# A hybrid decoder layer on one core: a narrow group norm, early small loads, and the sample's third score part moved forward

## The reference

```
sp = einsum('bqhcd,bkhcd->bhcqk', q, k_past) * ATT_SCALE      # sample: 1024 past keys out of pages
sn = einsum('bqhcd,bkhcd->bhcqk', q, k) * ATT_SCALE           # and 4 new ones
p = softmax(concatenate([sp, sn], axis=-1), axis=-1)
wgt = p[:, :, 0] - lam * p[:, :, 1]                           # differential attention, prompt and sample alike
o = einsum('bhqk,bkhd->bqhd', wgt, v)
o_att = rmsnorm(o, g_subln) * (1.0 - lam_init)
...
mean = mean(y, axis=-1)                                       # y: (tokens, 8 heads, 64) of the RWKV group
var = mean(square(y - mean), axis=-1)
y = ((y - mean) * rsqrt(var + GN_EPS)).reshape(b, t, D_RWKV)
y = y * ln_x_w + ln_x_b
y = (y + bonus) * g
mix = concatenate([o_att, y], axis=-1) @ w_o
```

## Time and profile before

| | us |
|---|---|
| runs | 2062.02, 2064.7, 2070.59 |
| median | 2064.7 |
| the profiled execution's own time | 2063.8 |
| its span, first to last instruction | 2062.0 |
| TensorE busy in the span | 1852.0 |
| VectorE busy | 1078.5 |
| ScalarE busy | 810.7 |
| GpSimd busy | 292.7 |

### The profile page before, as it was taken

The page is one execution under the profiler, slowest core; times in us unless marked ns, Lnnn a source line. Parts: engine busy times, 40 slices in busy tenths (PEclk is TensorE's granted clock), DMA queues, the critical chain, the costliest instruction groups (busy, mean ns, idle before and its releaser), DMA issues.

```text
span 2062.0 us, 45942 instructions
## 1 busy us (share of the span) xinstructions
PE 1852.0 (90%) x19468; PEld 1752.3 (85%) x19468; DVE 1078.5 (52%) x1790; ACT 810.7 (39%) x1438; POOL 292.7 (14%) x292
## 2 busy tenths in 40 slices
PE   5999999699998588884397999999999999999996
PEld 5988888599997466662397999999999999999996
DVE  4355544345445455545736577553337766532654
ACT  4242323022232266652234554543335555432442
POOL 0011111059971000002100000000000000000000
PEclk9999999899999688886699999999999999999997
DMA  4233333530012677534133343323434422333442
GB/s 153 99 124 128 132 119 135 194 110 3 3 26 45 192 215 196 152 103 169 41 103 134 104 144 129 100 89 118 137 113 153 146 92 93 99 111 106 121 139 95
DMA packets 100140, 240.71 MB, mean 117 GB/s; under 512 B 14243, under 2 KB 18467, under 8 KB 99651
## 3 DMA queue, kind: packets, MB, share of 16 engines
q1 hardware_dynamic: 99362, 235.63, 35.9%
q10 hardware_dynamic: 576, 2.16, 0.3%
HBM read 189.54 MB, written 48.21 MB: 115 GB/s over the span
## 4 chain that ended last, share of the span: by engine, by line
PE 47%; DVE 2%; ACT 1%; issue 1%; DMA 0%; POOL 0%; SPq 0%; ACTq 0%; DVEq 0%
PE tl_acc L2096 45%; PE tl_ple L2096 1%; PE tl_wide L2070 0%; PE tl_wide L2061 0%; DVE tl_tmp L2369 0%; DVE tl_gated L2431 0%; DVE tl_gated L2434 0%; ACT tl_sq_e L2108 0%; ACT tl_wh L2245 0%; DVE tl_Y L2351 0%; DVE tl_Y L2342 0%; ACT tl_Hh L2214 0%; DVE tl_acc_e L2275 0%; DMA tl_xt<-dram_xT 0%; ACT tl_Y L2194 0%
## 5 line engine op out<-in xcount | busy, mean ns | idle before, releaser
L2096 PE MATMUL tl_acc<-tl_Hh,tl_wh 128*128 128x264 f32 x1536 | 438.5, 285 | 7.4 <-DVE tl_Hl L2373 7.4
L2096 PE MATMUL tl_acc<-tl_Hh,tl_wl 128*128 128x264 f32 x1536 | 438.1, 285 | 0.0
L2096 PE MATMUL tl_acc<-tl_Hl,tl_wh 128*128 128x264 f32 x1536 | 436.1, 284 | 0.0
L2415 DVE TENSOR_TENSOR tl_wl<-tl_raw,tl_wh 128x1024 fp32r<-128x1024 f32 (+2 forms) x182 | 206.0, 1132 | 418.7 <-ACT tl_wh L2245 418.5
L2245 ACT ACTIVATE tl_wh<-tl_raw 128x1024 fp32r<-128x1024 f32 (+2 forms) x182 | 178.9, 983 | 497.1 <-PE tl_acc L2096 455.9
L2096 PEld LDWEIGHTS tl_acc<-tl_Hh,tl_wh 128*128 128x128 f32 x1536 | 290.0, 189 | 8.7 <-DVE tl_Hl L2373 8.4
L2096 PEld LDWEIGHTS tl_acc<-tl_Hl,tl_wh 128*128 128x128 f32 x1536 | 290.3, 189 | 0.0
L2096 PEld LDWEIGHTS tl_acc<-tl_Hh,tl_wl 128*128 128x128 f32 x1536 | 290.1, 189 | 0.0
L2096 PE MATMUL tl_acc<-tl_Gl,tl_wh 128*128 128x264 f32 x704 | 200.4, 285 | 0.0
L2096 PE MATMUL tl_acc<-tl_Gh,tl_wl 128*128 128x264 f32 x704 | 200.3, 284 | 0.0
L2096 PE MATMUL tl_acc<-tl_Gh,tl_wh 128*128 128x264 f32 x704 | 200.1, 284 | 0.0
(11 more groups left out here) (360 smaller groups left out, 4458.2 us busy)
## 6 DMA issues: line engine op xcount, KB each, us to landing
tl_raw<-dram_w_up SPq DMA_DIRECT2D x88, 512.0 KB, 3.6
as_kT<-dram_k_pool SPq DMA_DIRECT2D x64, 256.0 KB, 3.1
as_vp<-dram_v_pool SPq DMA_DIRECT2D x64, 256.0 KB, 3.0
tl_raw<-dram_w_down SPq DMA_DIRECT2D x32, 448.0 KB, 3.4
dram_projT<-fr_cur SPq DMA_DIRECT2D x26, 528.0 KB, 2.9
fr_raw<-dram_w_in SPq DMA_DIRECT2D x52, 256.0 KB, 3.6
tl_raw<-dram_w_pg SPq DMA_DIRECT2D x32, 320.0 KB, 3.2
ap_dup<-dram_projT SPq DMA_DIRECT2D x16, 512.0 KB, 8.9
```

Of the source, the lines that this page charges most:

```text
L2096: last = nc.tensor.matmul(out[:, n, 0:HP], w[:, u % 2, k, :], z, start=(begin and q == 0), stop=(end and q == 2))
L2415: tt(wl[:, u % 2, 0:kt], raw[:, u % 3, 0:kt], wh[:, u % 2, 0:kt].bitcast(F32), ALU.subtract).then_inc(S["residued"], 1)
```

## The change

Three parts. (1) The finish computes one row of variances for each head and third of the tokens, with a matrix of 32 columns for each pair (`var_cols`), accumulates all four pairs into one PSUM tile, takes the root and the reciprocal once on 96x352, and spreads the result back to 64 rows with `var_rows`. The means have two PSUM tiles. The bias is added on ScalarE. The block matrices are loaded in the scan, the attention's outputs are loaded first. (2) The values of head 0, the table and the small pieces of the attention are loaded in the scan (`early`); in the attention the queries and keys of head 1 are issued first. (3) In the orders of the attention, part 2 of a sample's scores goes to the end of the step with s % 4 = 2, its copy ahead of the next `exponential`, the sample's maximum to right behind `peak`, its exponential to right behind the next `exponential`; the split of the next head begins one tile earlier; the end of the last head is done in 7 + 1 tiles with the samples' rows apart.

```
@@ attend: SP @@
-            sp.dma_start(table[:], a["table"]).then_inc(Z["table_in"], 16)
-            load_v(0)
-            for j in range(3):
-                sp.dma_start(qkv[:, j], ...).then_inc(Z["small_in"], 16)
-            sp.dma_start(mask[:], a["new_mask"]).then_inc(Z["small_in"], 16)
-            sp.dma_start(comb[:, 0:17], a["comb"]).then_inc(Z["small_in"], 16)
-            sp.wait_ge(Z["table_in"], 16)
+            load_qk(1)
             for g in range(3):
                 keys(0, g)
             values(0)
...
-                if s % NQ == 0 and h + 1 < HEADS:
+                if s % NQ == 0 and 0 < h and h + 1 < HEADS:
                     load_qk(h + 1)
...
                 if s % 4 == 2 and n + 1 < NB:
-                    keys(n + 1, 0)
-                    keys(n + 1, 1)
-                if s % 4 == 3 and n + 1 < NB:
-                    keys(n + 1, 2)
+                    for g in range(3):
+                        keys(n + 1, g)
...
-            store(HEADS - 1)
             sp.wait_ge(Z["out_kept"], 1)
             sp.dma_start(oT.rearrange("h p t -> p h t")[:, :, SEQ:T], out_s[:]).then_inc(Z["stored"], 16)
+            store(HEADS - 1)
+            sp.wait_ge(S["o_kept"], HEADS + 1)
+            sp.dma_start(oT[HEADS - 1][:, SEQ - P:SEQ], out[:, SEQ - P:SEQ]).then_inc(S["o_stored"], 16)
@@ attend: GpSimd, TensorE (turn_new) @@
-            pool.wait_ge(Z["small_in"], 16 * 5)
-                pe.wait_ge(Z["small_in"], 16 * 5)
@@ attend: TensorE's order @@
                 if s < U:
                     score(s)
-                if s % 4 == 3 and n < NB:
-                    sample_scores(n, 2)
...
                     sample_scores(n, 1)
                 if s >= 3:
                     values(s - 3)
+                if s % 4 == 2 and n < NB:
+                    sample_scores(n, 2)
@@ attend: VectorE's order @@
                     peak(s)
+                if s % 4 == 3 and n < NB:
+                    sample_peak(n)
                 if s % 4 == 0 and 1 <= n:
                     sample_combine(n - 1)
...
                     norm_rows(s // NQ - 1)
-                if s % 4 == 3 and n < NB:
-                    sample_peak(n)
-                if s % NQ >= NQ - 4 and s // NQ + 1 < HEADS:
-                    low(s // NQ + 1, s % NQ - (NQ - 4))
+                if NQ - 5 <= s % NQ < NQ - 1 and s // NQ + 1 < HEADS:
+                    low(s // NQ + 1, s % NQ - (NQ - 5))
@@ attend: ScalarE's order; high() one tile earlier as well @@
+                if s % 4 == 3 and n < NB:
+                    sample_move(n, 2)
                 if s < U:
                     exponential(s)
                 if s % 4 == 3 and n < NB:
-                    sample_move(n, 2)
+                    sample_exp(n)
                 if 2 <= s < U + 2:
                     keep(s - 2)
...
-                if s % NQ == 2 and s >= NQ:
+                if s % NQ == 2 and NQ <= s < U:
                     root_rows(s // NQ - 1)
-                if s % 4 == 3 and n < NB:
-                    sample_exp(n)
+                if s == U + 1:
+                    act.wait_ge(Z["squared"], NB)
+                    nc.scalar.activation(rms[:, 2], rms[:, 2], ACT.Sqrt, bias=eps, scale=1.0 / P).then_inc(Z["rooted"], 1)
+                    root_rows(HEADS - 1)
...
+            root_rows(HEADS)
             keep_rows(HEADS - 1)
+            act.wait_ge(S["o_turned"], HEADS + 1)
+            nc.scalar.activation(out[:, SEQ - P:SEQ], pv[:, 0:P], ACT.Copy, scale=gs[:]).then_inc(S["o_kept"], 1)
@@ rwkv_scan: SP, behind the loads of before @@
+            for dst, src in early:
+                sp.dma_start(dst, src).then_inc(S["early_in"], 16)
+            sp.wait_ge(S["early_in"], 16 * len(early))
             sp.wait_ge(S["state"], NCH)
@@ finish_rows: TensorE @@
+            def var(p):
+                pe.wait_ge(S["squared"], p + 1)
+                for n in range(3):
+                    last = nc.tensor.matmul(pr[group(n), 0:T3], var_cols[:, p, :], sq[:, p % 2, n * T3:(n + 1) * T3],
+                                            start=(p == 0), stop=(p == NPAIR - 1), skip_group_check=True)
+                last.then_inc(S["var"], 1)
+
+            def spread(p):
+                if p >= 2:
+                    pe.wait_ge(S["scaled"], p - 1)
+                for n in range(3):
+                    last = nc.tensor.matmul(wide[p % 2][:, n, 0:T3], var_rows[group(n), p, :], rstd[group(n), :],
+                                            start=True, stop=True)
+                last.then_inc(S["spread"], 1)
             mean(0)
+            mean(1)
             for p in range(NPAIR):
...
+                var(p)
+                if p + 2 < NPAIR:
+                    mean(p + 2)
+            pe.wait_ge(S["inverted"], 1)
+            pe.wait_ge(S["centred"], NPAIR)
+            for p in range(NPAIR):
+                spread(p)
@@ finish_rows: ScalarE, behind the squares @@
+            act.wait_ge(S["var"], NPAIR)
+            nc.scalar.activation(rstd[0:ROWS], pr[0:ROWS, 0:T3], ACT.Sqrt, bias=epsg[0:ROWS]).then_inc(S["rooted"], 1)
+            o_high(HEADS - 1)
+            for p in range(NPAIR):
+                shift(p)
@@ finish_rows: VectorE @@
-                nc.vector.reciprocal(sd[:, p % 2], sd[:, p % 2]).then_inc(S["inverted"], 1)
-                tt(dev[:, p], dev[:, p], sd[:, p % 2], ALU.mult).then_inc(S["divided"], 1)
+                dve.wait_ge(S["spread"], p + 1)
+                tt(part(dev[:, p]), part(dev[:, p]), wide[p % 2][:, :, 0:T3], ALU.mult).then_inc(S["scaled"], 1)
...
             centre(3)
             o_low(2)
+            dve.wait_ge(S["rooted"], 1)
+            nc.vector.reciprocal(rstd[0:ROWS], rstd[0:ROWS]).then_inc(S["inverted"], 1)
+            o_low(3)
+            scale(0)
+            scale(1)
+            residue(0)
+            low(0)
             scale(2)
+            residue(1)
+            low(1)
             scale(3)
+            low(2)
+            low(3)
```

More of the change, by code:

```diff
@@ L873, in turn_v @@
                 h = s // NQ
[L874 removed]
+                if h:
+                    pe.wait_ge(S["v_in"], h * 16)
                 if s >= NQ:
@@ L1155, in leave, with root_rows @@
                     .then_inc(S["evacuated"], 1)
[L1157 to L1162 removed]
+            def root_rows(part):
+                g, n = (part % 2, slice(0, NQ)) if part < HEADS - 1 else (1, slice(0, NQ - 1)) if part == HEADS - 1 \
+                    else (1, slice(NQ - 1, NQ))
+                act.wait_ge(S["squared"], NQ * (part + 1) if part < HEADS - 1 else U - 1 + part - (HEADS - 1))
+                nc.scalar.activation(rms[:, g, n], rms[:, g, n], ACT.Sqrt, bias=eps, scale=1.0 / P)\
                     .then_inc(S["rooted"], 1)
@@ L1688, in square @@
                 nc.scalar.activation(sq[:, p % 2], dev[:, p], ACT.Square).then_inc(S["squared"], 1)
-            def root(p):
-                act.wait_ge(S["var"], p + 1)
-                if p >= 2:
-                    act.wait_ge(S["divided"], p - 1)
-                nc.scalar.activation(part(sd[:, p % 2]), pq[:, :, 0:T3], ACT.Sqrt, bias=epsg).then_inc(S["rooted"], 1)
             def high(p):
```

154 lines of the change are left out of this document (75 added, 79 removed).

## The result

The changed kernel takes **2038.26 us** (median of 4 runs, 2034.51 to 2040.27) against 2064.23 for the kernel before on the same chip: ratio 0.987, 95% interval 0.984 to 0.989. The forecast was 2032 with a range of 2016 to 2048, so the side and the range held. The gain is 26.0 us where the sum had 31.8, and the sum's parts held less well than its total: the finish gave somewhat more, and the attention almost nothing, because the reorderings took its other gains back.

What follows compares the result with a forecast made beforehand. VectorE's list bounds the finish, a chain between engines the attention; the tail gives nothing back. Minus 23.7, minus 5, minus 7.2, plus 6.6, minus 2.5 make minus 31.8: from 2063.8 to 2032 us, range 2016 to 2048.

Steps and rivals of the forecast that it cites:

- Finish: Stage after attention: one narrow root and reciprocal instead of four wide ones; 72.9 to 49.2 us, minus 23.7.
- The replay by instruction: New finish followed instruction by instruction from its start: last variance 16.1, reciprocal 19.1, spread 20.4, tail 49.2 us.
- Start and first head: Attention's beginning: early loads remove TensorE waits, but sample pages come late; minus 5 us, ends 0 and minus 13.
- A new wait of 9 us: Before the first sample scores: TensorE waits for pages queued behind the second head's load.
- Boundaries: Between heads, three times: shorter waits and two thirds of a full clock's gain; minus 2.4 us each, minus 7.2.
- near 797.2: Between heads: when ScalarE's copy of turned tile 13 is done, so turn 14 starts there instead of at 797.5.
- the new gaps are 1.3 and 1.6 us: Between heads: TensorE's waits in the new order, where one of 4.07 us stood.
- Middles: Steps 2 to 4 of heads 1 to 3: reorderings delay the sample turn; plus 2.2 us each, plus 6.6.
- End: Attention's end: root's table load and most of the norm no longer follow the last tile; minus 2.5 us.
- the last sample's delay: Attention's end: the delay seen in the heads' middles costs 1.7 us at the last sample too.
- the attention gives nothing: Rival for the attention: the clock drops as before, only the finish's gain remains; 2041 us, chance 0.25.
- the finish gains only half: Rival for the finish: VectorE and GpSimd collide, spread without overlap, 12 us less; about 2052 us, chance 0.05.

Runs made afterwards that it cites:

- finish_alone: The kernel before with only the narrow finish, its three small matrices loaded in the scan; attention as before: 2039.52 us.
- gate_dve: The changed kernel with the finish's four gating multiplies on VectorE instead of GpSimd: 2033.64 us.
- head1_scan: The changed kernel with head 1's queries and keys loaded in the scan, so the sample's pages come first in attention: 2032.71 us.
- orders_back: The changed kernel with the sample scores' third part and the next head's splitting put back in their old places: 2032.41 us.
- third_back: The changed kernel with only the sample scores' third part, its maximum and exponential put back; early splitting stays: 2035.16 us.
- split_back: The changed kernel with only the next head's splitting put back; the sample scores' third part stays early: 2038.67 us.
- fill: The changed kernel with extra unread products on TensorE where it waits in the attention: 2023.64 us.

## Why the prediction was right, and where it was wrong

**Finish: right in mechanism and nearly in size.** Predicted minus 23.7, measured minus 25.5, and all of it the finish's own (finish_alone). The replay by instruction held: last variance over at 15.1 us after the first mean (forecast 16.1), reciprocal at 18.1 (19.1), first scale at 19.8 (20.4), tail at 47.2 (49.2). The variance took 0.79 us for three products (0.85 taken), the spread 1.55 (1.3 taken); both bounds had been 0.85 and 1.94. The Trainium skill's rule that a change of tiling mode drains TensorE (TensorEngine Tiling (Array Packing), Key Properties), weighed there, is not to be seen in the six changes from the first mean to the last spread (the prediction counted eight): the variance begins at 948.12 where the mean before it ends, and the next mean at 948.84, though the ends are modelled. One step of the replay doesn't add up: two means of 3.89 us end at 7.9, not "near 7.2". They ended at 6.5, with a mean granted clock of 0.58 up to there and of 1.00 in the 9 us behind. The stalls against GpSimd, which the replay laid out one by one, were there (the first long low part ended 30.7 us after the first mean, forecast 30.6), and gate_dve showed what the sharing was worth: 3.7 us.

**Start and first head: right in mechanism, short in size.** "A new wait of 9 us" came as 9.65, and head1_scan took it away with its cause. The early loads alone were worth more than the 5 I gave them: 61.4 to 53.5 us in orders_back. In the changed kernel 2.5 were left, because the reorderings took 5.4 back; I had costed them in the later heads only.

**Boundaries: the step that failed.** It had minus 7.2, about two thirds of the 3.4 us per boundary that a full clock would give. The rest of the three heads, which holds the boundaries, took 113.1 us before and 116.1 after (113.0 and 113.1 in two other profiles of its order): nothing was gained. Two things were wrong in the step. First the chain: I had the copy of turned tile 13 end "near 797.2"; it ended at 799.71. The third part waits 1.31 us for ScalarE, and the sample's maximum stands behind both maxima of tile 15 on VectorE, so its exponential began at 797.74 and held that copy, and the turn behind it, until 799.85. Second the clock: "the new gaps are 1.3 and 1.6 us" was right (1.31 and 1.69), but that shorter gaps would hold the clock was only hoped, and it fell to 0.52. The price itself was right by luck. Its working has the sample turn at "some 3.3" us behind the wait; the trace of before has 3.69, and the proportion gives 4.1 with the one and 4.9 with the other, not 3.4. With the clock held the three stretches were 3.5, 4.4 and 3.1 us shorter (in the one shown 10.9 to 6.5).

```profile
799.03 3.69 PE L951 MATMUL as_one<-as_combs,as_prob 128*128 128x16 f32 x18
```

**Middles: right in mechanism and size, for two of three.** Plus 2.2 each was forecast, for three. The middles of heads 1 and 2 took 2.1 us more each (19.15 to 21.21), that of head 3 nothing: the term counted a splitting there, but head 3 has no next head. It is the splitting that costs (third_back); the third part, which the term also counted with 0.85, adds 0.4 in all three together (split_back, 57.9). The rounding ahead of the sample's third copy and the low part ahead of maximum 12 stand where the prediction put them:

```profile
763.25 1.04 ACT L1104 ACTIVATE ap_qs<-ap_dup 128x1024 fp32r<-128x1024 f32 x1
...
768.59 1.22 DVE L995 TENSOR_TENSOR ap_qs<-ap_dup,ap_qs 64x1024 fp32r<-64x1024 f32 x1
...
769.84 0.82 DVE L1005 TENSOR_REDUCE ap_small<-ap_sc 128x1 f32<-128x640 f32 x1
...
772.42 0.82 PE L938 MATMUL as_one<-as_combs,as_prob 128*128 128x16 f32 x3 [1.96 <-DVE as_combs L1053]
```

**End: minus 4.2 without the last sample's delay, measured minus 6.1** (32.8 to 22.8, of which 3.9 are the finish's).

**The sum.** Reorderings, with the delay at the last sample: forecast plus 1.1. Measured against orders_back in the traces: plus 5.4 in the first head, where nothing had been counted, plus 4.1 in the middles and minus 2.4 to plus 0.7 in the rest, so plus 7 to plus 10; in the totals 5.9. Early loads and the attention's end were undersized by 3 and 2 us and the finish by 2, and these make up for most of it: that the total lies within the range is to that extent luck. The result lies nearer to the rival *the attention gives nothing* (2041) than to the forecast; but that rival too had the clock as its whole reason, and the clock falls in either order, while the early splitting costs by its chain. (The rival *the finish gains only half* was added up wrongly: 12 us less than the forecast is 2044, not 2052.)

## What to carry to other kernels

A wait removed on the engine that works most may be worth nothing: here its 12.2 us went, and the time stayed. Ask which instruction the new order puts ahead of the copy that this engine needs next, on each of the other engines. When a stretch behind a wait runs at the lower granted clock, shortening the wait is a gamble; extra products of no use, written to a part of a PSUM bank that the engine owns at that moment, held the clock here and were worth 12 to 15 us, where the prediction gave the boundaries 11 at most. Count them to the wait: too many in the middles cost 3.3 us. And a load moved ahead of others in a queue should be costed with what then stands behind it.

## What the runs showed of the hardware that was not expected

- Extra TensorE work made the program faster: 466 products of 128 columns, 28.8 us of TensorE's time in the run fill, took 14.6 us off the total. The Trainium skill (TensorE: Matmul & The Clock Gate, Part 1: The HAM clock gate) has activity lift the clock from its lower level; the windows at 1.00 instead of 0.52 agree.
- A small store issued 9 us behind a 2 MB load landed 4.4 to 5.4 us after its issue instead of 1.7 to 2.1, from the load's queue and from another engine's alike. The step into the next block, which waits for it, took 5.0 to 6.0 us instead of 2.3 to 2.8.
- GpSimd's multiply is held up as well as VectorE: 2.49 us for the first gate and 3.26 to 3.29 for the others in the changed kernel. Each of the longer ones began 0.2 us behind a VectorE instruction with two operands in SBUF (967.77, 974.81 and 981.87), the first one beside one with an operand in PSUM.
